# Softmax weights turned in 32x32 blocks on VectorE, value products in eight 32x64 tiles, and more low parts added by transfers

## The reference, cut to what matters

```python
sc = jnp.einsum("bqhgd,bkhd->bhgqk", q_blk, k_blk).astype(jnp.float32) * scale
m = jnp.maximum(jnp.max(sc, axis=-1, keepdims=True), sink_b)
p = jnp.exp(sc - m)
denom = jnp.sum(p, axis=-1, keepdims=True) + jnp.exp(sink_b - m)
probs = (p / denom).astype(v_blk.dtype)
return jnp.einsum("bhgqk,bkhd->bqhgd", probs, v_blk)
```

## Time and profile before

| | |
|---|---|
| median of 3 runs | 1304.26 us |
| the profiled execution itself | 1304.11 us |
| its span in the profile | 1302.3 us |
| PE busy in the span | 1290.0 us, 99% |
| DVE, ACT, POOL busy | 799.6, 604.0, 113.7 us |
| mean granted TensorE clock | 0.998 of full |

### The profile page before, as it was taken

How to read it: one execution, slowest core, us unless ns; L and a number is a source line. 1 busy time by engine, 2 the same in 40 slices (tenths; PEclk the granted TensorE clock), 3 DMA queues, 4 the chain that set the end, 5 groups by cost and what they waited for, 6 DMA issues and landing times.

```text
span 1302.3 us, 16405 instructions
## 1 busy us (share of the span) xinstructions
PE 1290.0 (99%) x6688; PEld 1065.7 (82%) x6688; DVE 799.6 (61%) x1087; ACT 604.0 (46%) x897; POOL 113.7 (9%) x109
## 2 busy tenths in 40 slices
PE   9999999999999999999999999999999999999997
PEld 8877777889888888888898777888888888888886
DVE  7888798866444444342378987979654444443425
ACT  6765766436333333311286667653453333332112
POOL 2023511001000000000020334100000000000000
PEclk9999999999999999999999999999999999999999
DMA  5422466523333333423143216663233333334332
GB/s 200 156 65 66 97 135 132 187 64 115 98 97 97 97 97 97 129 97 98 53 137 127 65 50 141 126 187 115 80 104 95 96 98 98 98 95 128 97 97 112
DMA packets 36954, 140.77 MB, mean 108 GB/s; under 512 B 4144, under 2 KB 4560, under 8 KB 35728
## 3 DMA queue, kind: packets, MB, share of 16 engines
q1 hardware_dynamic: 33552, 127.91, 30.8%
q0 software_dynamic: 3328, 11.82, 5.4%
HBM read 133.42 MB, written 6.29 MB: 107 GB/s over the span
## 4 chain that ended last, share of the span: by engine, by line
PE 95%; DVE 2%; ACT 1%; issue 0%; POOL 0%; DMA 0%; DVEq 0%
PE ps L873 18%; PE ps L875 18%; PE ps L874 18%; PE ps L1010 9%; PE ps L1011 9%; PE ps L1012 9%; PE ps L899 5%; PE ps L1223 2%; PE ps L1237 1%; PE ps L1247 1%; PE ps L1257 1%; PE ps L1002 1%; PE ps L1170 1%; PE ps L1207 0%; PE ps L1196 0%
## 5 line engine op out<-in xcount | busy, mean ns | idle before, releaser
L873 PE MATMUL ps<-hhi,whi 128*128 128x512 f32 x1040 | 409.5, 394 | 0.0
L875 PE MATMUL ps<-hhi,wlo 128*128 128x512 f32 x1040 | 405.1, 390 | 0.0
L874 PE MATMUL ps<-hlo,whi 128*128 128x512 f32 x1040 | 404.8, 389 | 0.0
L622 ACT ACTIVATE whi<-raw 128x1024 fp32r<-128x1024 f32 x208 | 219.3, 1056 | 219.3 <-DMA raw<-in_units 219.3
L1315 DVE TENSOR_TENSOR wlo<-raw,whi 128x1024 fp32r<-128x1024 f32 x186 | 227.3, 1224 | 149.9 <-ACT whi L622 149.9
L873 PEld LDWEIGHTS ps<-hhi,whi 128*128 128x128 f32 x1040 | 195.2, 188 | 44.2 <-issue 4.9
L875 PEld LDWEIGHTS ps<-hhi,wlo 128*128 128x128 f32 x1040 | 195.2, 188 | 41.2
L874 PEld LDWEIGHTS ps<-hlo,whi 128*128 128x128 f32 x1040 | 195.3, 188 | 39.7
L1010 PE MATMUL ps<-whi,uhi 128*128 128x512 f32 x352 | 137.1, 390 | 0.0
L1012 PE MATMUL ps<-wlo,uhi 128*128 128x512 f32 x352 | 137.0, 389 | 0.0
L1011 PE MATMUL ps<-whi,ulo 128*128 128x512 f32 x352 | 136.9, 389 | 0.0
(11 more groups left out here) (184 smaller groups left out, 1525.1 us busy)
## 6 DMA issues: line engine op xcount, KB each, us to landing
raw<-in_units SPq DMA_DIRECT2D x208, 512.0 KB, 3.7
wlo<-in_units POOLq DMA_DIRECT2D x22, 512.0 KB, 5.7
gb<-in_gb SPq DMA_DIRECT2D x5, 1024.0 KB, 5.8
h_kept<-hb SPq DMA_DIRECT2D x2, 2048.0 KB, 9.2
ha<-h_kept SPq DMA_DIRECT2D x2, 2048.0 KB, 9.8
hb<-in_x SPq DMA_DIRECT2D x4, 512.0 KB, 5.8
out_y<-hb SPq DMA_DIRECT2D x8, 256.0 KB, 2.0
cn<-in_cn SPq DMA_DIRECT2D x1, 663.5 KB, 10.2
```

What stands on the lines that cost most here:

```text
L622: A(whi[:, m % RING, :], raw[:, m % RING, :], ACT.Copy).then_inc(unit_hi, 1)
L873: mm(out, whi[:, slot, cols], xhi, start=start, stop=False)
L874: mm(out, whi[:, slot, cols], xlo, start=False, stop=False)
L875: return mm(out, wlo[:, slot, cols], xhi, start=False, stop=stop)
```

## The change

Five things change. First, `AP` goes and `PT` moves from ACT to DVE: one 32x32-block transposing copy of the 128x1024 weights a round, from `sc` to `p_t` in SBUF. Turned in blocks, the keys of a 128-row tile stand in four groups of 32 partitions (by query block of 32). So, second, the values are spread: 16 transfers of 64 KB a layer on SP copy `v_tm` to `v_rep`, in which each group of 32 partitions holds all the keys. Third, `AV` becomes 64 matmuls a block of 32 rows by 64 columns by 128 moving columns (two rounds, two heads, 32 queries), in eight tiles, four PSUM banks (4 to 7) and two column halves. Fourth, it moves: it runs between the first and the second half of the matmuls of unit 8 + 2t + 3 (units 11, 13, 15, 17), where it stood behind the scores of that stage, and it takes both aux banks. Fifth, `BY_DMA` grows from units 20 to 30 to units 12 to 30, so that DVE no longer splits units 12 to 19. Some steps of the scan at units 17 and 18 (`SE`) move by a place.

```diff
-BY_DMA = range(20, 31)
+BY_DMA = range(12, 31)
+SQ = 32
+AV_AT = {A0 + 2 * t + 3: t for t in range(NBLK)}
@@ mixer_schedule
+        if n in AV_AT:
+            steps += [("AV", AV_AT[n])]
         steps += [("G", n), ("E", n)]
+        if n == 18:
+            steps += [("SE", 0)]
...
-        if i in (3, 5, 7):
-            steps += [("AV", (i - 3) // 2)]
...
-        if 0 <= i - 1 < 8:
-            steps += [("AP", i - 1)]
...
@@ banks
+                aux(("AV", i, "first"), [(al_done, 4, i + 1)], False)
                 aux(("AV", i), [(al_done, 4, i + 1)])
@@ SP, before the load of unit 13
+                    if n == U_CONV + RING:
+                        sp_eng.wait_ge(v_done, L + 1)
+                        sp_eng.wait_ge(own_done, L * 2 + 2)
+                        for a in range(P // SQ):
+                            for q in range(BLK // SQ):
+                                sp_eng.dma_start(v_rep[a * SQ:(a + 1) * SQ, q::BLK // SQ, :],
+                                                 v_tm[q * SQ:(q + 1) * SQ, :, :]).then_inc(v_spread, 16)
@@ PE
+            def values(L, t):
+                pe.wait_ge(v_spread, (L + 1) * 256)
+                pe.wait_ge(pt_done, L * 8 + 2 * t + 2)
+                wait_aux_free(pe, L, ("AV", t, "first"))
+                wait_aux_free(pe, L, ("AV", t))
+                if t:
+                    pe.wait_ge(al_done, L * 4 + t)
+                blocks = SEQ // SQ
+                for kb in range(blocks):
+                    for a in range(P // SQ):
+                        rows = slice(a * SQ, (a + 1) * SQ)
+                        for g in range(2):
+                            last = mm(ps[g * HEAD:(g + 1) * HEAD, 4 + a, 0:QPK * SQ],
+                                      v_rep[rows, (t // 2) * blocks + kb, g * HEAD:(g + 1) * HEAD],
+                                      p_t[t % 2][rows, :, kb, 2 * g:2 * g + 2, :],
+                                      start=kb == 0, stop=kb == blocks - 1, skip_group_check=True)
+                last.then_inc(aux_full, 1)
...
-                            pe.wait_ge(pt_done, L * 8 + 8)
+                            pe.wait_ge(al_done, L * 4 + 4)
...
@@ DVE
+                    elif what == "PT":
+                        t, m = ATTN[i]
+                        dve.wait_ge(as_norm, 2 * (L * 8 + i) + 2)
+                        if t >= 2:
+                            wait_aux_full(dve, L, ("AV", t - 2))
+                        V.transpose(p_t[t % 2][:, m, :, :, :].rearrange("p k j q -> p j k q"),
+                                    sc[i % 2][:].rearrange("p j (k q) -> p j k q", q=SQ)).then_inc(pt_done, 1)
```

More of the change, by code:

```diff
@@ L11 @@
 from contextlib import ExitStack
+import functools
 import numpy as np
@@ L146, in mixer_schedule @@
         if n == 18:
[L147 removed]
+            steps += [("SE", 1), ("SF", 0)]
         if U_CONV <= n < U_Z:
@@ L151, in mixer_schedule @@
                 steps += [("SIL2", n - U_CONV)]
+            if n == 18:
+                steps += [("SE", 2)]
             if n == 17:
@@ L160, in mixer_schedule @@
         if n == 17:
-            steps += [("SB", 0), ("SE", 0), ("SC", 0)]
+            steps += [("SB", 0), ("SC", 0)]
         elif a >= 0:
@@ L265, in trunk @@
         zt = at("zt", 32, [P, TOK])
-        sc = [at("sc0", 34, [P, QPK, SEQ]), at("sc1", 0, [P, QPK, SEQ], start=base_h)]
-        p_t = [at("p_t0", 38, [P, 2, 512]), at("p_t1", 4, [P, 2, 512], start=base_h)]
+        sc = [at("sc0", 34, [P, QPK, SEQ]), at("sc1", 38, [P, QPK, SEQ])]
+        v_rep = at("v_rep", 90, [P, TOK // SQ, P])
+        p_t = [at("p_t0", 98, [P, 2, SEQ // SQ, QPK, SQ]), at("p_t1", 0, [P, 2, SEQ // SQ, QPK, SQ], start=base_h)]
         cv = at("cv", 8, [P, 2, TOK], start=base_h)
@@ L805, in _ @@
                         A(ast[:, i % 2, 4, :], ast[:, i % 2, 2, :], ACT.Exp).then_inc(as_exp, 1)
[L806 to L812, removed]
                     elif what == "AV":
                         wait_aux_full(act, L, ("AV", i))
-                        A(ahi[:, 0:QPK, i * BLK:(i + 1) * BLK],
-                          ps[:, aux_bank(("AV", i)), :].rearrange("p (j q) -> p j q", q=BLK),
-                          ACT.Copy).then_inc(ah_done, 1)
+                        A(ahi[:, 0:QPK, i * BLK:(i + 1) * BLK].rearrange("p j (a q) -> p a j q", q=SQ),
+                          ps[:, 4:8, 0:QPK * SQ].rearrange("p a (j q) -> p a j q", q=SQ), ACT.Copy).then_inc(ah_done, 1)
                     elif what == "SQ":
@@ L875, in three, with by_columns @@
                 return mm(out, wlo[:, slot, cols], xhi, start=False, stop=stop)
-            def by_columns(slot, bank):
+            def by_columns(slot, bank, between=None):
                 for c in range(CT):
+                    if between and c == CT // 2:
+                        between()
                     last = three(ps[:, bank, :], slot, slice(c * P, (c + 1) * P), hhi[:, c, :], hlo[:, c, :],
@@ L1088, in _ @@
                         wait_split(pe, unit(L, i))
-                        by_columns(unit(L, i) % RING, unit_bank(i))
+                        between = functools.partial(values, L, AV_AT[i]) if i in AV_AT else None
+                        by_columns(unit(L, i) % RING, unit_bank(i), between)
                     elif what == "G":
@@ L1241, in _ @@
                         last.then_inc(as_full, 1)
[L1242 to L1253, removed]
-                        for m in range(2):
-                            for kt in range(2):
-                                for g in range(2):
-                                    last = mm(ps[g * HEAD:(g + 1) * HEAD, aux_bank((what, i)), m * 2 * BLK:(m + 1) * 2 * BLK],
-                                              v_tm[:, (i // 2) * 2 + kt, g * HEAD:(g + 1) * HEAD],
-                                              p_t[m][:, kt, g * 2 * BLK:(g + 1) * 2 * BLK],
-                                              start=(kt == 0), stop=(kt == 1), skip_group_check=True)
-                        last.then_inc(aux_full, 1)
                     elif what == "RS":
```

37 lines of the change are left out of this document (11 added, 26 removed).

## The result

The changed kernel takes 1323.24 us (median of 4 runs, 1322.07 to 1324.57) where the kernel before takes 1304.24; the ratio is 1.0146, with a 95% interval of 1.0134 to 1.0159. The forecast was 1323.5 us. The profiled execution took 1322.07 us; its span is 1320.3 us, where it was 1302.3.

A forecast was written before the change was run, and what follows sets the result against it. PE, busy 99% of the span, was taken to bound the kernel; +9.6 us a layer, +19.2 in both, on a span of 1302.3 plus 1.8 around it gave 1323.3, put at 1323.5 us, 8 in 10 from 1308 to 1343.

The forecast's parts named there:

- to the end of the scores of round 3: First stretch of a layer: block 0 waits for the copy of round 1; scores end at 94.1 for 90.33, +3.3 us.
- round 3 to round 5: `T` waits for `SIL2` until 9.0, products wait 3.5 us for the `CB` bank; 23.3 us for 18.30, +5.0.
- round 5 to round 7: `T` waits for `SIL2` until 8.4, products wait 3.5 us again; 22.8 us for 19.63, +3.2.
- round 7 to the end of `T`: No round follows, so 8.4 + 0.44 us and a mode change: 9.1 us for 11.0, -1.9.
- from there to the stage of unit 20: Products 1.1 us longer but half a unit earlier, which takes away the old 1.1 us wait: 0.
- The two lengths: On DVE from the end of the scores: 7.63 us until `CB` is out of its bank, 8.36 until `SIL2` is done.
- a slow copy: Rival: DVE's transposing copy takes twice the split, 2.44 us, adding 19.5 us, 1343 us in all; chance 0.14.
- row groups that don't overlap: Rival: the value products gain nothing from four row groups, 8 x 4.6 us more, 1360 us; chance 0.05.
- the waits don't form: Rival: DVE empties the bank before PE is there, so the kernel gets 7.3 us faster, 1297 us; chance 0.07.
- the lower end: Low end of the value products' range, 1.9 us a block if four row groups gave all; forecast used 3.0.
- The clock: Rival: PE's clock falls to 1.2 GHz in four new waits of 3.5 us, +11 us, 1334 us; chance 0.06.
- the 16.3 us of `AP`: PE time freed by dropping 16 transposes of 1.02 us each; claimed to be used up by waits.

The follow-up runs named there:

- e1: Changed kernel with the value products, and their evacuation, back behind the scores of their stage: 1305.01 us.
- e4: Changed kernel with DVE's `CB` copy moved behind the transposing copy and ACT's copy of `T` moved ahead of the exponentials: 1313.03 us.
- e10: Changed kernel with the value products in PSUM banks 2 to 5, shared with the scores, in place of 4 to 7: 1309.37 us.
- e7: Changed kernel with 12 unread filler multiplications on PE ahead of the value products of blocks 1 and 2: 1320.46 us.
- e2: Changed kernel with only DVE's `CB` copy moved, to right behind the transposing copy: 1324.0 us.
- e6: Changed kernel with the low parts of units 12 to 19 computed on DVE again, without the added transfers and ACT's negations: 1347.13 us.
- e9: Kernel before with only `BY_DMA` grown to units 12 to 30: 1304.12 us.
- e8: Changed kernel with ACT taking `CB` out and copying `T` ahead of its exponentials, `T` of units 11 to 15 and the products placed later: 1297.80 us.
- e12: Changed kernel with each block's 64 matmuls reordered, two row groups at a time, four tiles in work in place of eight: 1341.63 us.

## Why the prediction was right

The forecast, 1323.5 us, stands 0.3 us from the median. Its steps against layer 0 of the profile, whose chain has these pieces (start us, us):

```profile
92.34 1.09 PE ps L1247 x8
...
115.13 1.09 PE ps L1247 x8
...
139.01 1.09 PE ps L1247 x8
...
148.56 0.66 PE ps L1172 x4
```

and on PE's timeline the stage of unit 20 begins:

```profile
171.04 0.50 PE L861 MATMUL ps<-hhi,whi 128*128 128x512 f32 x1
```

| step | forecast | measured |
|---|---|---|
| to the end of the scores of round 3 | +3.3 | 93.43 for 90.33, +3.1 |
| round 3 to round 5 | 23.3 (+5.0) | 22.8 (+4.5) |
| round 5 to round 7 | 22.8 (+3.2) | 23.9 (+4.3) |
| round 7 to the end of `T` | 9.1 (-1.9) | 9.1 (-1.9) |
| from there to the stage of unit 20 | 22.9 (0) | 21.8 (-1.0) |

The sum is +8.9 in this layer (171.04 for the 162.13 of the earlier trace rows) for a forecast of +9.6, and 18.0 in both for 19.2. (The starts of the chain's scores have 1.09 us added for their ends, that of `T` 0.66.)

**Right by its mechanism.** The two lengths taken from DVE's timeline before held. `T` of unit 11 begins 8.98 us after the scores of round 3 (102.41; forecast 9.0), and the `CB` bank is empty 16.4 us after them (109.84; forecast 16.5). The waits in the middle of units 13 and 15 were put at 3.5 us and are 3.42, 3.44, 3.41 and 1.86. e1, e4 and e10 take them away in three ways, by place, by earlier copies and by other banks, and 18, 10 and 14 us go with them. The copy was put at 1.22 us, from the split of the same size, and takes 1.24; in layer 0 block 0 begins at 87.31 where 87.3 was worked out. The rivals of a slow copy and of row groups that don't overlap fall with these durations (1.24 us a copy, 2.08 us a block), and the rival that the waits don't form falls with the waits.

**The products were mis-sized.** They were put at 3.0 us; six blocks took 2.1, below the 2.2 at which the prediction called itself wrong. 0.44 us of four large tiles, with their filling and draining, was too short a burst to take a rate from; the lower end, 1.9 us, was the better one. The other two terms of the 3.0 us, 0.1 us for filling and draining and 0.2 us for the change of mode, were read from no row. The second shows as the 0.2 us by which each half unit behind the products is longer than 2.74 (89.39 to 92.34), so that 2.3 us stand against 3.0. That this left the total in place is chance in part. On the other side stand 0.25 us from DVE's `CB` copy to the first product, 0.5 us that I took off the first step for the missing `AP` though DVE held that time (the copy of round 1 ended at 87.21, as the split had), and the clock, which in two blocks of eight made 3.4 to 3.7 us of 2.1.

**The clock was a rival and came in part.** The prediction had it fall in all four waits at a price of 11 us, or not at all. It fell behind two of them, at a price of 1.7 us each (e7), and behind some waits for SIL2, where the next wait can hide it. The share of the clock in the 19 us was not measured as a whole.

**Two sentences mislead.** "In the old place [...] nothing waited" is true of the kernel before, and I took it to hold for the new products there too: with both aux banks taken, the old place makes `T` and `CB` wait for the result's low part, 9.2 us (e1), and the version reaches 1305 us, not the 1290 that I worked out from the sentence. And the wait was put down to DVE, whose copy ends last; it has two causes within 0.44 us of each other. The prediction named `t_evac` beside `cb_done` but gave it no time. Moving the one copy that it had priced (e2) gained nothing.

**What it took to cost nothing.** PE waits for none of the 38 transfers of low parts (5.5 us each to landing) and, as far as the waits show, for none of the transfers that spread the values (block 0 begins 0.1 us after DVE's copy):

```profile
wlo<-in_units POOLq DMA_DIRECT2D x38, 512.0 KB, 5.5
...
v_rep<-v_tm SPq DMA_DIRECT2D x32, 64.0 KB, 2.1
```

But "costs nothing" was half of it: beside the copies on DVE this part saves 24 us (e6), in the kernel before nothing (e9).

**Where the 16.3 us of `AP` are.** e8 finds some: with most waits gone, the kernel is 6.4 us faster than the one before. The products take back 8 x 0.2 us, and the half units behind them about as much again. 2.6 us are PE waiting for DVE's taps in units 10 and 11, where DVE goes without a gap every 7.43 us and most of what `AP` leaves can't be used; 1.7 us are waits for SIL2. The rest was not measured.

## What to carry to other kernels

Work taken from the bounding engine is worth only what the next engine's stage leaves. So set the two stages side by side first: here DVE's 8.4 us against PE's 5.49 + 1.06 + 0.44 + 0.87 and half a block of products, 8.9. A consumer that takes two buffers waits for the later of two copies. When their ends lie close together the table of waits shows one of them, and moving that one alone gains nothing: here 0 and 0 us for one each, 10.2 us for both. Moving an instruction ahead of the work that hid its wait cost 18 us here (e1). Moving its neighbour `T` behind such work and the products two eighths of a unit later, with both copies early, turned the loss into a gain of 6.4 us (e8).

## What the runs showed of the hardware

- A transposing copy in 32x32 blocks of 128x1024 float32, SBUF to SBUF, takes 1.24 us on DVE, as long as a subtraction of that size. The Trainium skill ("VectorE: DVE Perf Modes", The three transpose paths) has 311 ns for 128x128 in bf16, from which the prediction estimated 2.5 us; the measurement decides, it is half of that.
- 128 records of matmuls in eight 32x64 tiles take 2.08 us, 16.3 ns each; in four tiles at a time 26 ns (e12). With two records to a matmul that is 32.5 ns a matmul. The Trainium skill's floor of about 25 ns from start to start ("TensorE: Matmul & The Clock Gate", Part 1) holds for the mean if it counts matmuls and not if it counts records; the runs don't say which it counts. Between single starts it isn't kept: the first eight records of block 0 start within 0.07 us. The 4 ns that the Trainium skill has between packed tiles (Part 3 of the same page) are nearer to that, but the mean over the 128 is four times as long.
- PE's clock fell to the lower level behind some waits of 2.3 to 3.6 us and not behind others of the same length: 3.42 us at 110 without, 3.44 at 132 with. No run settles what decides it. With filler in the wait the products of all four blocks ran at full clock (2.08 to 2.09 us), and the version without such waits (e8) has 0.999 granted.
- A fall of the clock costs nothing where a longer wait follows: behind the wait for SIL2 that ends at 753.89 `T` and much of the half unit ran at the lower clock (0.50 granted from 753.8 to 756.6), the next wait was 1.86 us in place of 3.42, and the products began as long after `T` as in the other layer.
